# Block inversion of the delta rule's triangular systems: moving operands of 64 columns, last level on blocks of 64

## The reference

```python
def gated_delta_chunked(q, k, v, g, beta):
    ...
    decay = jnp.where(incl, jnp.exp(diff), 0.0)
    kb = k * beta[..., None]
    a = jnp.where(strict, jnp.einsum('bhnid,bhnjd->bhnij', kb, k) * decay, 0.0)
    rhs = jnp.concatenate([v * beta[..., None], kb * jnp.exp(G)[..., None]], axis=-1)
    sol = lax.linalg.triangular_solve(a, rhs, left_side=True, lower=True, unit_diagonal=True)
    u, w = sol[..., :DV], sol[..., DV:]
    ...
```

## Time and profile before

| | us |
|---|---|
| median of three runs | 2311.2 (2310.29 to 2311.8) |
| the profiled execution | 2310.71 |
| its span | 2308.9 |
| TensorE matmul busy in it | 2069.1 (90%) |
| VectorE, ScalarE, GpSimd busy | 1335.6, 881.3, 70.9 |
| the inversion, first mask to last subtraction | 1442.10 to 1580.60 |

### The profile page before, as it was taken

The page is one execution under the profiler, slowest core; times in us unless marked ns, Lnnn a source line. Parts: engine busy times, 40 slices in busy tenths (PEclk is TensorE's granted clock), DMA queues, the critical chain, the costliest instruction groups (busy, mean ns, idle before and its releaser), DMA issues. The chain is left out here.

```text
span 2308.9 us, 34519 instructions
## 1 busy us (share of the span) xinstructions
PE 2069.1 (90%) x14388; PEld 1924.2 (83%) x14388; DVE 1335.6 (58%) x2047; ACT 881.3 (38%) x1092; POOL 70.9 (3%) x60
## 2 busy tenths in 40 slices
PE   4987888999999999999997997998699967778997
PEld 4987787899999998888886894998599967557997
DVE  4545673799888886555555955554455423333643
ACT  4345442244443334444444435122154323223532
POOL 0000000000000000000000000551000000000000
PEclk8998998999999999999998989999799988788999
DMA  4442344354444445555553331000255545403553
GB/s 155 165 150 92 110 148 162 128 183 149 160 149 147 147 147 198 187 197 191 190 200 122 145 114 58 1 1 1 73 180 183 184 111 192 142 31 129 182 183 119
DMA packets 50949, 317.89 MB, mean 138 GB/s; under 512 B 5202, under 2 KB 10322, under 8 KB 14212
## 3 DMA queue, kind: packets, MB, share of 16 engines
q1 hardware_dynamic: 50244, 315.48, 38.7%
q10 hardware_dynamic: 576, 0.55, 0.1%
HBM read 309.20 MB, written 6.82 MB: 137 GB/s over the span
## 5 line engine op out<-in xcount | busy, mean ns | idle before, releaser
L294 DVE TENSOR_TENSOR s_ring_lo<-s_ring,s_w_hi 128x2048 fp32r<-128x2048 f32 x263 | 602.4, 2291 | 430.1 <-ACT s_w_hi L288 429.5
L288 ACT ACTIVATE s_w_hi<-s_ring 128x2048 fp32r<-128x2048 f32 x263 | 501.1, 1906 | 257.1 <-PE bank L2108 105.7
L331 PE MATMUL bank<-s_hT_hi,s_w_hi 128*128 128x256 f32 x2320 | 343.6, 292 | 38.2 <-ACT s_w_hi L288 30.8
L331 PEld LDWEIGHTS bank<-s_hT_hi,s_w_hi 128*128 128x128 f32 x2320 | 308.9, 198 | 47.3 <-issue 47.3
L331 PE MATMUL bank<-s_hT_hi,s_ring_lo 128*128 128x256 f32 x2320 | 330.9, 286 | 7.0 <-DVE s_ring_lo L294 6.9
L331 PEld LDWEIGHTS bank<-s_hT_hi,s_ring_lo 128*128 128x128 f32 x2320 | 304.4, 195 | 8.2 <-DVE s_ring_lo L294 8.2
L1204 PE MATMUL bank<-s_w_hi,s_hT_lo 128*128 128x512 f32 x1024 | 242.6, 389 | 0.3 <-issue 0.3
L1204 PEld LDWEIGHTS bank<-s_w_hi,s_hT_lo 128*128 128x128 f32 x1024 | 192.2, 188 | 40.3 <-issue 0.4
L331 PE MATMUL bank<-s_hT_lo,s_w_hi 128*128 128x256 f32 x1296 | 190.3, 292 | 0.0
L331 PEld LDWEIGHTS bank<-s_hT_lo,s_w_hi 128*128 128x128 f32 x1296 | 175.9, 201 | 0.0
L331 PE MATMUL bank<-s_x_r,s_w_hi 128*128 128x256 f32 x1024 | 144.5, 284 | 0.0
(11 more groups left out here) (316 smaller groups left out, 2565.0 us busy)
## 6 DMA issues: line engine op xcount, KB each, us to landing
s_ring<-weights SPq DMA_DIRECT2D x282, 1024.0 KB, 4.8
bias_by_distance<-s_arena SPq DMA_DIRECT2D x1, 4608.0 KB
s_arena<-bias_by_distance SPq DMA_DIRECT2D x12, 384.0 KB, 4.1
s_arena<-consts SPq DMA_DIRECT2D x1, 1792.0 KB, 8.5
s_x<-x SPq DMA_DIRECT2D x1, 1024.0 KB, 7.0
s_arena<-mem SPq DMA_DIRECT2D x1, 1024.0 KB, 10.2
x_away<-s_x SPq DMA_DIRECT2D x1, 1024.0 KB, 4.8
s_arena<-sub_keys SPq DMA_DIRECT2D x1, 1024.0 KB, 7.3
```

What stands on the lines that cost most here:

```text
L288: act.activation(k.w_hi[:, u % 2, :], k.ring[:, u % RING, :], ACT.Copy).then_inc(k.hi_ready, 1)
L294: dve.tensor_tensor(k.ring_lo[:, u % RING, :], k.ring[:, u % RING, :], plain(k.w_hi[:, u % 2, :]), ALU.subtract).then_inc(k.lo_ready, 1)
L331: last = pe.matmul(out[:, nb * S:(nb + 1) * S], w[:, c, nb * P:(nb + 1) * P], h[:, c, :], start=(n == 0 and c == 0), stop=(n == 2 and c == 7))
```

## The change

Y has a zero block in one corner before the last level: until then the 128x128 inverse consists of two diagonal blocks of 64. The change stores these two side by side, `y_side`, 128 partitions by 64 columns a system, and `eye_side` is the identity in that form.

- Levels 0 to 5: the first product and the delta of Y move 64 columns a system in place of 128. The stationary operands stay 128x128. The delta of X needs z as stationary operand, with its blocks in place, so ScalarE writes z twice: side by side (`z_side`, one activation) and on the diagonal (`z_diag`, two activations of 64 partitions). `z_diag`'s other corners are zeroed once at the start.
- Level 6: only one 64x64 block of the inverse is new in each system. Both products run on 64 rows and 64 columns: operands are cut from `g.A` and X directly, without a mask. ScalarE first copies `y_side` into `g.Y`; VectorE writes the new block with its sign changed, and zeroes the opposite one.
- GpSimd makes no mask for level 6, and the masks' table loses that level, so one DMA in `gdn_build` brings 24 blocks of 128x128 in place of 28.
- A semaphore `zeros_ready` holds TensorE's level-0 products and ScalarE until VectorE has zeroed `z_diag` and written `eye_side`.

The diff of `gdn_invert`; the rest is the size of the masks' table in four places, and `g.at_stacked`, the free place behind it:

```diff
@@ -1837,17 +1838,22 @@
 
 
     g, ps, H = k.gdn, k.ps, GDN_H
-    TOGETHER, LEVELS = 4, 7
+    TOGETHER, LEVELS, Q = 4, 7, P // 2
     am = carve(k, 0, TOGETHER, 4, P)
-    zs = carve(k, g.at_v, 2, 4, P)
-    names = ("level_ready", "z_mm", "z_out", "delta_mm", "y_ready", "x_ready")
-    level_ready, z_mm, z_out, delta_mm, y_ready, x_ready = (ctx_sem(k, n) for n in names)
+    lay = Layout(k, g.at_v)
+    z_diag, z_side, eye_side = lay.take(2, 4, P), lay.take(2, 4, Q), lay.take(Q)
+    y_side = carve(k, g.at_stacked, TOGETHER, 4, Q)
+    names = ("level_ready", "z_mm", "z_out", "delta_mm", "y_ready", "x_ready", "zeros_ready")
+    level_ready, z_mm, z_out, delta_mm, y_ready, x_ready, zeros_ready = (ctx_sem(k, n) for n in names)
+    low, high = slice(0, Q), slice(Q, P)
+
...
             for s in steps:
+                if s.level == LEVELS - 1:
+                    continue
                 if s.n >= TOGETHER:
                     last = steps[s.n - TOGETHER]
                     pool.wait_ge(z_mm, last.n + 1)
@@ -1880,22 +1892,9 @@
 
         @block.tensor
         def _(pe):
-            def delta(s):
-                pe.wait_ge(z_out, s.deltas)
-                pe.wait_ge(y_ready, s.n - 1)
-                pe.wait_ge(x_ready, steps[s.n - 2].xs)
-                for c in range(4):
-                    last = pe.matmul(ps[2 + s.n % 2][:, c * P:(c + 1) * P], g.X[:, s.h, c, :], zs[:, s.n % 2, c, :],
-                                     start=True, stop=True)
-                if s.level < LEVELS - 1:
-                    for c in range(4):
-                        last = pe.matmul(ps[4 + s.n % 2][:, c * P:(c + 1) * P], zs[:, s.n % 2, c, :],
-                                         g.X[:, s.h, c, :], start=True, stop=True)
-                last.then_inc(delta_mm, 1)
-
-            before = None
-            for s in steps:
-                pe.wait_ge(level_ready, s.n + 1)
+            def first(s):
+
+                bank = ps[s.n % 2]
                 if s.n >= 2:
                     if steps[s.n - 2].level == 0:
                         pe.wait_ge(y_ready, s.n - 1)
@@ -1903,12 +1902,45 @@
                         pe.wait_ge(z_out, steps[s.n - 2].deltas)
                 if s.level > 0:
                     pe.wait_ge(y_ready, s.n - TOGETHER + 1)
+                if s.level == LEVELS - 1:
+                    for to, systems, source in halves_of:
+                        for c in range(systems.start, systems.stop):
+                            last = pe.matmul(bank[to, c * Q:(c + 1) * Q], g.A[source, s.h, c, to],
+                                             y_side[source, s.h % TOGETHER, c, :], start=True, stop=True)
+                    last.then_inc(z_mm, 1)
+                    return
+                pe.wait_ge(level_ready, s.masked)
+                if s.level == 0:
+                    pe.wait_ge(zeros_ready, 1)
                 for c in range(4):
-
-                    y = k.ident if s.level == 0 else g.Y[:, s.h, c, :]
-                    last = pe.matmul(ps[s.n % 2][:, c * P:(c + 1) * P], am[:, s.h % TOGETHER, c, :], y,
+                    y = eye_side if s.level == 0 else y_side[:, s.h % TOGETHER, c, :]
+                    last = pe.matmul(bank[:, c * Q:(c + 1) * Q], am[:, s.h % TOGETHER, c, :], y,
                                      start=True, stop=True)
                 last.then_inc(z_mm, 1)
+
+            def delta(s):
+                pe.wait_ge(z_out, s.deltas)
+                pe.wait_ge(y_ready, s.n - 1)
+                pe.wait_ge(x_ready, steps[s.n - 2].xs)
+                bank = ps[2 + s.n % 2]
+                if s.level == LEVELS - 1:
+                    for to, systems, _ in halves_of:
+                        for c in range(systems.start, systems.stop):
+                            last = pe.matmul(bank[to, c * Q:(c + 1) * Q], g.X[to, s.h, c, to],
+                                             z_side[to, s.n % 2, c, :], start=True, stop=True)
+                    last.then_inc(delta_mm, 1)
+                    return
+                for c in range(4):
+                    pe.matmul(bank[:, c * Q:(c + 1) * Q], g.X[:, s.h, c, :], z_side[:, s.n % 2, c, :],
+                              start=True, stop=True)
+                for c in range(4):
+                    last = pe.matmul(ps[4 + s.n % 2][:, c * P:(c + 1) * P], z_diag[:, s.n % 2, c, :],
+                                     g.X[:, s.h, c, :], start=True, stop=True)
+                last.then_inc(delta_mm, 1)
+
+            before = None
+            for s in steps:
+                first(s)
                 if before is not None:
                     delta(before)
                 before = s if s.level > 0 else None
@@ -1916,27 +1948,55 @@
 
         @block.scalar
         def _(act):
+            act.wait_ge(zeros_ready, 1)
             for s in steps:
-                if s.level > 0:
-                    act.wait_ge(z_mm, s.n + 1)
-                    act.activation(all4(zs[:, s.n % 2]), ps[s.n % 2][:, :], ACT.Copy).then_inc(z_out, 1)
+                if s.level == 0:
+                    continue
+                act.wait_ge(z_mm, s.n + 1)
+                z = by_system(ps[s.n % 2], Q)
+                if s.level == LEVELS - 1:
+                    act.wait_ge(y_ready, s.n - TOGETHER + 1)
+                    for to, _, _ in halves_of:
+                        act.activation(g.Y[to, s.h, :, to], y_side[to, s.h % TOGETHER], ACT.Copy)
+                    for to, systems, _ in halves_of:
+                        last = act.activation(z_side[to, s.n % 2, systems, :], z[to, systems, :], ACT.Copy)
+                    last.then_inc(z_out, 1)
+                    continue
+                act.activation(z_side[:, s.n % 2], z, ACT.Copy)
+                for to, _, _ in halves_of:
+                    last = act.activation(z_diag[to, s.n % 2, :, to], z[to], ACT.Copy)
+                last.then_inc(z_out, 1)
 
         @block.vector
         def _(dve):
             eye = k.ident.rearrange("p (s n) -> p s n", s=1).to_broadcast([P, 4, P])
+            for to, systems, other in halves_of:
+                dve.memset(z_diag[to, 0, :, other], 0.0)
+                dve.memset(z_diag[to, 1, :, other], 0.0)
+            for to, _, _ in halves_of:
+                last = dve.tensor_copy(eye_side[to, :], k.ident[to, to])
+            last.then_inc(zeros_ready, 1)
+            dve.wait_ge(zeros_ready, 1)
+            eyes = eye_side.rearrange("p (s n) -> p s n", s=1).to_broadcast([P, 4, Q])
             for s in steps:
+                y = y_side[:, s.h % TOGETHER]
                 if s.level == 0:
                     dve.wait_ge(z_mm, s.n + 1)
-                    dve.tensor_tensor(g.Y[:, s.h], eye, ps[s.n % 2][:, :].rearrange("p (s n) -> p s n", s=4),
-                                      ALU.subtract).then_inc(y_ready, 1)
+                    dve.tensor_tensor(y, eyes, by_system(ps[s.n % 2], Q), ALU.subtract).then_inc(y_ready, 1)
                     dve.tensor_tensor(g.X[:, s.h], eye, am[:, s.h % TOGETHER], ALU.subtract).then_inc(x_ready, 1)
                     continue
                 dve.wait_ge(delta_mm, s.deltas)
-                dve.tensor_tensor(all4(g.Y[:, s.h]), all4(g.Y[:, s.h]), ps[2 + s.n % 2][:, :], ALU.subtract)\
-                   .then_inc(y_ready, 1)
-                if s.level < LEVELS - 1:
-                    dve.tensor_tensor(all4(g.X[:, s.h]), all4(g.X[:, s.h]), ps[4 + s.n % 2][:, :], ALU.subtract)\
-                       .then_inc(x_ready, 1)
+                d = by_system(ps[2 + s.n % 2], Q)
+                if s.level == LEVELS - 1:
+                    for to, systems, other in halves_of:
+                        last = dve.tensor_scalar(g.Y[to, s.h, systems, other], d[to, systems, :], -1.0, None, ALU.mult)
+                    last.then_inc(y_ready, 1)
+                    for to, systems, other in halves_of:
+                        dve.memset(g.Y[other, s.h, systems, to], 0.0)
+                    continue
+                dve.tensor_tensor(y, y, d, ALU.subtract).then_inc(y_ready, 1)
+                dve.tensor_tensor(all4(g.X[:, s.h]), all4(g.X[:, s.h]), ps[4 + s.n % 2][:, :], ALU.subtract)\
+                   .then_inc(x_ready, 1)
 
 
 def gdn_recur(k):
```

19 lines of the change are left out of this document (12 added, 7 removed).

## The result

The changed kernel took 2315.23 us (median of 13 runs, 2314.02 to 2319.41), the kernel before 2311.6 (13 runs, 2310.29 to 2313.42). The ratio is 1.0018, with a 95% interval of 1.0009 to 1.0026. The kernel became about 0.2% slower. I had forecast 2306.3, in a range of 2302 to 2314. The profiled execution took 2315.01 us, with a span of 2313.2 (before: 2308.9).

A forecast was written before the change was run, and what follows sets the result against it. The prediction took TensorE, paced by its weight loads, as the inversion's bound. Last level -5.0, level 0 -0.55, start +0.4 and end +0.25 gave -4.9 us against the 2311.2 median: 2306.3 us, range 2302 to 2314.

The forecast's parts named there:

- Pace of levels 1 to 5: Levels 1 to 5: weight loads keep a pair at 112 ns and a step at 2.68 us, gain 0.
- ScalarE, VectorE, GpSimd in levels 1 to 5: Levels 1 to 5: ScalarE's extra copies and VectorE's shorter subtraction stay hidden behind TensorE, 0 us.
- The falling clock: Rivals in which TensorE's granted clock drops, at the start or seams (0.24) or inside levels 1 to 5 (0.09).
- dips at the start or the seams: Rival: late copies, or one or two clock dips of about 2 us in level 0 or 64x64 blocks; 2307 to 2314, chance 0.24.
- the clock falls inside levels 1 to 5: Rival: narrower work lowers the clock, 2.1 us more per step, up to 2390 us; above 2316, chance 0.09.
- Last level: Level 6: 64-column loads save 0.45 us a block, ScalarE's rounds then limit; -5.0 us, ends 0 and -7.1.
- ScalarE's round: Last level: four activations, 1.15 us from first product's end to the delta, three such rounds counted per group.
- Drains between tiling modes: Last level: about ten mode changes; at 0.275 us per drain the gain would be up to 2.8 us smaller.
- Level 0: Level 0: VectorE and GpSimd alternate, 1.96 us a head; only each group's last y comes earlier, -0.55 us for both.
- Start: Stage start: TensorE's first product waits for VectorE's zeroing and identity copies, +0.4 us; far end 3.7 us later.
- The end: After the last delta: two scalings and two memsets replace one subtraction, +0.25 us, up to +0.7.
- my cases: Forecast 0.52, start or seams 0.24, no last-level gain 0.06, moving operand 0.09, falling clock 0.09; last two outside the range.

The follow-up runs named there:

- e10_before_narrow: The kernel before, with the first product and the delta of Y moving only 64 of 128 columns in levels 1 to 5: 2319.53 us, ratio 1.0027.
- e8_pad128: The changed kernel with 128-column level 0, no TensorE wait for zeros_ready, and three of four 64-column products in levels 1 to 5 padded to 128: 2311.13 us.
- e6_y_behind: The changed kernel with ScalarE's two copies of Y placed behind its copies of z in three of four last-level steps: 2317.24 us, ratio 1.0024.
- e12_no_y: The changed kernel without ScalarE's two copies of Y's diagonal blocks in the last level: 2316.40 us, ratio 1.0016.
- e9_whole_last: The changed kernel with last-level products on whole 128x128 weight loads again, GpSimd clearing A's diagonal blocks in place: 2320.56 us, ratio 1.0034.
- e3_fill: The changed kernel with unread filler products in TensorE's gaps, before the first product and in levels 0 and 6: 2309.77 us, ratio 1.0006.

## Why the prediction was wrong, point by point

**Pace of levels 1 to 5.** Right. A pair keeps 112 ns with 64 columns, a step 2.68 us; the weight load sets it. The Trainium skill, TensorE: Matmul & The Clock Gate, prices a product by its moving columns (Back-to-back issue gap) and a load by its own (LDWEIGHTS); after, e10_before_narrow and e8_pad128 show the second alone deciding, at 64 and at 128 moving columns.

**ScalarE, VectorE, GpSimd in levels 1 to 5.** Right: hidden, B and E moved by 0.09 us.

**The step that failed.** I priced half the moving columns at zero because the pace doesn't change, and carried over the granted clock of 1.00 from the earlier trace rows to a kernel that moves less. For level 0 I even wrote that no row shows a clock there, and still took it to be unchanged. The falling clock stood among the rivals twice. As dips at the start or the seams it had a price of about 2 us each and 0.24; measured are 4.2, 2.9 and 1.9. As "the clock falls inside levels 1 to 5" it had 0.09, and my argument against it was that the blocks follow without a gap. That is true in the middle of the levels, where the clock held. It doesn't hold in the first steps of level 1, ahead of which TensorE idles for 0.95 and 0.99 us: e10_before_narrow shows the fall there, with nothing changed for TensorE but the columns, and e8_pad128 undoes most of it with the columns alone. The price worked out there, about 2.1 us for a step at the low level, was a little small: 2.68 us became 5.12 for a step wholly at that level, 2.4 more, as a pair takes 213 ns there (1.71 us for eight) and I had 200. The places are three, and few steps each.

**Last level.** Its mechanism was right, its size was not: -5.0 forecast, -2.8 measured (C and F, the end included). The blocks are cheaper than I took: eight loads span 0.32 us, and where loads of L1908 and L1929 run between each other's, both blocks together start within 0.23 us (1507.72 to 1507.95); I had 0.45 a block. ScalarE's round was the error: 1.43 us in place of 1.15. I had taken 0.26 between activations of 256 columns from the earlier trace rows, rows that read a bank; the copies of Y within s_arena take 0.42 each. And the round is not a latency that only three steps pay: it is a throughput, as e6_y_behind (order changed, nothing gained) and e12_no_y (copies left out, 2.1 us gained in the first group) show. Drains between tiling modes, which the Trainium skill (TensorEngine Tiling (Array Packing), Key Properties) warns of, were a lesser matter: the first block of 64 begins 0.20 us later than the pace asks (1505.35 in place of 1504.26 + 0.89), and so does the next one behind a full block (1507.72 in place of 1506.62 + 0.89). In e9_whole_last, without blocks of 64, the same place has no such delay. That it is a drain fits the page and isn't shown.

**Level 0.** VectorE and GpSimd still take turns, 1.96 us a head. With the clock up D falls by 0.25 us (e3_fill, 11.89 in place of 12.14); I had 0.27 a group.

**Start.** I took +0.4 us, with an end of +3.7. The first product came 1.4 us later, as VectorE's two copies of 64x64 took 1.36 us behind a mask, one mask and not four. The Trainium skill, SBUF — State Buffer, Who interferes with whom, has such a turn-taking lock, and the trace agrees: the copies end at 1442.49, just behind the second mask (1442.40). As cost in time this was nothing (e3_fill).

**The end.** It is inside F and can't be told apart; C and F differ in their gain by 0.8 us.

**The range.** It held four fifths of my cases, but I had let only one dip or two count, at 2 us, on a full gain. Three dips, 9.0 us in sum in the profiled execution, met a gain of 2.8.
